# A decoder layer with Strassen products: the up blocks of the feed-forward part taken product by product

## What is computed

```python
h = rmsnorm(x, pre_ffn_g[l])
up = causal_depthwise_conv(h @ w_up[l], conv_w[l], conv_b[l])   # w_up: 2048 x 2*5632, conv of 3 taps
gate, val = jnp.split(up, 2, axis=-1)
y = (jax.nn.gelu(gate, approximate=True) * val) @ w_down[l]     # w_down: 5632 x 2048
x = x + rmsnorm(y, post_ffn_g[l])
```

## Time and profile before

| | |
|---|---|
| median of 3 runs | 2533.48 us |
| profiled execution: its own time | 2530.21 us |
| profiled execution: span, first to last instruction | 2528.3 us |
| mean granted clock of TensorE | 0.999 |
| TensorE matmuls, busy | 15762, 2511.4 us (99%) |
| DVE busy | 2075.4 us (82%), 2517 instructions |
| ACT busy | 1333.5 us (53%), 1690 instructions |
| feed-forward stretch 1321.8 to 2391.8 | PE 1069.38, DVE 971.85, ACT 615.73 of 1070.00 us; DMA share 0.64 |

### The profile page before, as it was taken

How to read it: one execution, slowest core, us unless ns; L and a number is a source line. 1 busy time by engine, 2 the same in 40 slices (tenths; PEclk the granted TensorE clock), 3 DMA queues, 4 the chain that set the end, 5 groups by cost and what they waited for, 6 DMA issues and landing times. The chain is left out here.

```text
span 2528.3 us, 40321 instructions
## 1 busy us (share of the span) xinstructions
PE 2511.4 (99%) x15762; PEld 2271.4 (90%) x15762; DVE 2075.4 (82%) x2517; ACT 1333.5 (53%) x1690; POOL 185.0 (7%) x271
## 2 busy tenths in 40 slices
PE   9999999999999999999999999999999999999998
PEld 8888888888888888888999999999999999999997
DVE  8898888888888545436898989898999989898987
ACT  8554545555555322325555656555555555565544
POOL 0100000000000000000000101100000000001122
PEclk9999999999999999999999999999999999999999
DMA  6434343333344733434234566666666666666888
GB/s 253 151 124 143 124 136 113 109 121 117 103 158 132 291 99 126 157 128 173 75 101 167 167 175 173 177 173 172 176 165 166 167 166 161 166 167 160 257 234 290
DMA packets 106765, 405.42 MB, mean 160 GB/s; under 512 B 12432, under 2 KB 12448, under 8 KB 100960
## 3 DMA queue, kind: packets, MB, share of 16 engines
q1 hardware_dynamic: 72576, 263.76, 31.7%
q0 software_dynamic: 33728, 138.71, 21.4%
q10 hardware_dynamic: 288, 0.52, 0.1%
HBM read 303.33 MB, written 95.42 MB: 158 GB/s over the span
## 5 line engine op out<-in xcount | busy, mean ns | idle before, releaser
L922 PE MATMUL ps<-h_both,w_hl 128*128 128x256 f32 (+1 forms) x1360 | 416.3, 306 | 0.8 <-DVE w_hl L2777 0.8
L923 PE MATMUL ps<-h_both,w_hl 128*128 128x256 f32 (+1 forms) x1360 | 415.4, 305 | 0.0
L924 PE MATMUL ps<-h_both,w_hl 128*128 128x256 f32 (+1 forms) x1360 | 415.4, 305 | 0.0
L1813 ACT ACTIVATE w_hl<-w_raw 128x768 fp32r<-128x768 f32 x168 | 142.3, 847 | 339.6 <-PE ps L924 339.6
L1109 PE MATMUL ps<-rm_both,w_hl 128*128 128x512 f32 x896 | 315.4, 396 | 1.4 <-DVE w_hl L2262 0.8
L922 PEld LDWEIGHTS ps<-h_both,w_hl 128*128 128x128 f32 x1360 | 259.8, 191 | 13.5 <-DVE w_hl L2777 1.2
L924 PEld LDWEIGHTS ps<-h_both,w_hl 128*128 128x128 f32 x1360 | 259.8, 191 | 11.4
L923 PEld LDWEIGHTS ps<-h_both,w_hl 128*128 128x128 f32 x1360 | 259.9, 191 | 10.9
L922 PE MATMUL ps<-w_hl,h_both 128*128 128x512 f32 (+1 forms) x684 | 261.9, 383 | 1.1 <-issue 0.6
L923 PE MATMUL ps<-w_hl,h_both 128*128 128x512 f32 (+1 forms) x684 | 261.2, 382 | 0.0
L924 PE MATMUL ps<-w_hl,h_both 128*128 128x512 f32 (+1 forms) x684 | 261.0, 382 | 0.0
(11 more groups left out here) (387 smaller groups left out, 6462.7 us busy)
## 6 DMA issues: line engine op xcount, KB each, us to landing
w_raw<-in_w SPq DMA_DIRECT2D x487, 512.0 KB, 3.9
y_scratch<-work POOLq DMA_DIRECT2D x78, 512.0 KB, 9.6
y_scratch<-forms_f POOLq DMA_DIRECT2D x29, 512.0 KB, 13.3
y_scratch<-big POOLq DMA_DIRECT2D x27, 512.0 KB, 7.7
gate_scratch<-mixing POOLq DMA_DIRECT2D x8, 1024.0 KB, 6.0
mixing<-in_x POOLq DMA_DIRECT2D x4, 1024.0 KB, 7.0
mixing<-mixing POOLq DMA_DIRECT2D x16, 256.0 KB, 3.7
merged<-gate_scratch POOLq DMA_DIRECT2D x4, 1024.0 KB, 12.6
```

The lines of the kernel that those rows point to most:

```text
L922: pe.matmul(bank, s_hi, m_hi_, start=first, stop=False, skip_group_check=skip)
L923: pe.matmul(bank, s_hi, m_lo_, start=False, stop=False, skip_group_check=skip)
L924: return pe.matmul(bank, s_lo, m_hi_, start=False, stop=last, skip_group_check=skip)
L1813: act.activation(hi[:, 0:RAW_W], w_raw[:, i % RING, HB:], ACT.Copy).then_inc(hi_ready, 1)
```

## The change

The up blocks of subs 1 to 21 take the form of the W blocks, and with it the weight stream of these subs is packed as there (8 chunks of the same size: two of each quarter). A sub has 14 forms f = 0 to 13, in the order P1, Q5, Q6, Q3, Q7, P2, Q4, two of each product (half of the depth each); w_hl holds four forms, each good for 16 matmuls. `t_one` to `t_four` on DVE make the summed forms, of 1024 columns: into down_sum (SBUF) for the first half, and into bank pair 0 of PSUM for the second. ACT's `up_seed` copies x to y, and `up_half_*` copy out the left halves of the banks; DVE adds the right halves in eight steps. Form f + 4 takes the slot of form f.

Down block: the third sum goes to bank pair 0 and waits until ACT has taken product 1 out, not until product 3 is done; raw slots are given back by the right sum (two) and the third sum, not by the lo of k = 4 and 6; bank pairs and slots are renumbered. Plain down blocks use other banks for sub 21.

```diff
+            def up_half_form(s, f):
+                p, a, slot = CHAIN[f // 2], f % 2, slots_of(s)[f % RING]
...
+                pe.wait_ge(*up_lo_made(s, f))
+                if p == P1 and a == 0:
...
+                        pe.wait_ge(*pair_left(s, "x"))
...
+                if p == Q6 and a == 0:
+                    pe.wait_ge(up_seeded, s)
+                if p == Q3 and a == 0:
+                    pe.wait_ge(u_step, 6 * s - 5)
+                if p == Q7 and a == 0:
+                    pe.wait_ge(u_step, 6 * s - 4)
+                if p == Q4 and a == 0:
+                    pe.wait_ge(u_step, 6 * s - 2)
+                for kk in range(4):
...
+                    for m in range(2):
...
+                        pe.matmul(bank.rearrange("p (a s) -> p a s", a=2), w_hl[:, slot, 0, c], operand_both(p, k), ...)
+                        mm = pe.matmul(bank[:, 0:HB], w_hl[:, slot, 1, c], o_h, start=False, stop=k == KH - 1, ...)

 ACT
+            def up_half_q5(s):
+                act.wait_ge(*up_used(s, form_at(Q5, 1)))
+                act.wait_ge(v_tap0, s * 2)
+                act.activation(uc22, sum_halves(chain_banks(s)[2])[0], ACT.Copy).then_inc(up_half, 1)
...
+            def ups(s, tasks):
+                for f in range(2, FORMS):
+                    if f == 5:
+                        up_seed(s)
+                    if f == 7:
+                        up_half_q5(s)
+                    if f == 9:
+                        up_half_x2(s)
+                    up_hi(s, f)
+                    if f in tasks:
+                        tasks[f]()
+            def odd_tasks(g):
+                return {2: lambda: val_linear(g, 0), 5: lambda: gate_linear(g, 0), 9: lambda: gelus(2 * g)}
...
                 leave_product(g, e, 3)
-                sum_form_hi(g, e, 6)
-                quad_hi(c, PER_HALF, c + PER_HALF - 1)
-                quad_sum_hi(n + PER_HALF, PER_HALF)
+                sum_form_hi(s, 6)
+                up_hi(s + 1, 0)
                 leave_product(g, e, 4)
+                up_hi(s + 1, 1)
                 leave_product(g, e, 5)
-                quad_hi(c, PER_HALF + 1, c + PER_HALF)
-                quad_sum_hi(n + PER_HALF + 1, PER_HALF + 1)
                 leave_product(g, e, 6)
                 if e:
                     gate_linear(g, e)
+                    quad_half(g, 0, {2: lambda: val_linear(g - 1, 1), 4: lambda: gelus(2 * g - 1),
+                                     7: lambda: first_forms_hi(g - 1, half_chunk_0(g, 0)),
+                                     11: lambda: second_form_hi(g - 1), 12: lambda: third_forms_hi(g - 1)})

 DVE
+            def third_sum(s):
+                w = s - 2
+                dve.wait_ge(y_left, left_before(w) + 4)
+                dve.wait_ge(sum_ready, sums_before(s) + 2 + 6)
+                TTm(up_t[1], down_sum, down_raw(s, B21), ALU.subtract).then_inc(lo_ready, 1)
...
+            def ups(s, tasks, start=2):
+                for f in range(start, FORMS):
+                    if f == 7:
+                        up_q5(s)
+                    if f == 9:
+                        up_x2(s)
+                    if f == 11:
+                        up_c12_first(s)
+                    if f == 12:
+                        up_c22_first(s)
+                        up_c12(s)
+                        up_c22(s)
+                    up_lo_of(s, f)
+                    if f == 0:
+                        up_t_one(s, 0)
+                    if f == 2:
+                        up_t_one(s, 1)
+                    if f in (3, 4):
+                        up_t_two(s, f - 3)
+                    if f in (6, 7):
+                        up_t_three(s, f - 6)
+                    if f in (10, 11):
+                        up_t_four(s, f - 10)
+                    if f in tasks:
+                        tasks[f]()
+            def odd_tasks(g):
+                return {3: lambda: val_taps(g, 0, (1,)), 4: lambda: val_taps(g, 0, (0,)),
+                        6: lambda: gate_taps(g, 0, (1,)), 8: lambda: gate_taps(g, 0, (0,)),
+                        10: lambda: products(2 * g, 0)}
...
             def quad_half(g, e, tasks):
+                s = 2 * g + e
+                ups(s, tasks)
+                first_sum(s)
+                raw_form_lo(s, 0)
+                up_c11(s)
+                raw_form_lo(s, 1)
+                raw_form_lo(s, 2)
+                up_c21(s)
+                sum_form_lo(s, 3)
+                second_sum(s)
+                right_sum(s)
+                sum_form_lo(s, 4)
+                third_sum(s)
+                sum_form_lo(s, 5)
+                up_lo_of(s + 1, 0)
+                sum_form_lo(s, 6)
+                up_t_one(s + 1, 0)
+                up_lo_of(s + 1, 1)
                 if e:
                     gate_taps(g, e)
```

More of the change, by code:

```diff
@@ L112, in half_chunk_0, with up_base, downs_before, sums_before @@
     return C_LOOP + PER_HALF * half_index(g, e)
-def sums_before(g, e):
-    w = half_index(g, e)
-    return KH + PER_HALF * min(w, QUAD_HALVES) + KH * max(w - QUAD_HALVES, 0)
+def up_base(s):
+    return half_chunk_0(s // 2, s % 2) if s > 1 else C_SUB1
+def downs_before(s):
+    return min(max(s - 2, 0), QUAD_HALVES)
+def sums_before(s):
+    return 2 * (s - 1) + 6 * downs_before(s)
+def sum_his_before(s):
+    return 6 * (s - 1) + 4 * downs_before(s)
+def slots_of(s):
+    v = (0, 1, 2, 3)
+    for n in range(2, s + 1):
+        if n == 2 or n - 3 >= QUAD_HALVES:
+            v = v[2], v[3], v[0], v[1]
+        else:
+            v = v[3], v[2], v[0], v[1]
+    return v
+def down_slots(w):
+    v = slots_of(w + 2)
+    return v[2], v[3], v[0], v[1], v[2], v[0], v[1]
 def splits_before(g):
@@ L1963, in _ @@
                 r_split(2 * (j - RING), 2 * (j - RING) + 2)
-            for i in range(2):
-                quad_hi(C_SUB1, i, C_SUB1 - 2 + 2 * i)
-                quad_sum_hi(i, i)
-                if i == 0:
-                    act.wait_ge(r_lo, 4 * TT)
-                    for t in range(4):
-                        bank = done(A, FFN_USE, t, C_SUB1)
-                        dst = (u_gate, u_val)[t // 2][:, t % 2, :]
-                        act.activation(dst, bank, ACT.Copy).then_inc(plain_left, 1)
@@ L1974, in quads @@
-            def quads(c, n, tasks):
-                for i in range(2, KH):
-                    quad_hi(c, i, c + (i - 1))
-                    quad_sum_hi(n + i, i)
-                    if i in tasks:
-                        tasks[i]()
-            quads(C_SUB1, 0, {2: lambda: gate_linear(0, 0), 3: lambda: val_linear(0, 0), 4: lambda: gelus(0)})
-            quad_hi(C_LOOP, 0, C_LOOP - 1)
-            quad_sum_hi(KH, 0)
-            leave_p1(1)
-            quad_hi(C_LOOP, 1, C_LOOP)
-            quad_sum_hi(KH + 1, 1)
@@ new lines, in _ @@
+            up_hi(1, 1)
+            act.wait_ge(r_lo, 4 * TT)
+            for t in range(4):
+                bank = done(A, FFN_USE, t, C_SUB1)
+                dst = (u_gate, u_val)[t // 2][:, t % 2, :]
+                act.activation(dst, bank, ACT.Copy).then_inc(plain_left, 1)
+            def ups(s, tasks):
[9 more added lines that the diff above has]
+                        tasks[f]()
@@ L2820, in down_raw, with up_raw, up_lo_of @@
-            def down_raw(c, slot):
-                dve.wait_ge(raw_full[slot], (c // RING + KH // RING) * 16 + 16)
+            def up_raw(s, k):
+                c = up_base(s) + k
+                dve.wait_ge(raw_full[c % RING], c // RING * 16 + 16)
+                return w_raw[:, c % RING, :]
+            def up_lo_of(s, f):
+                p, slot = CHAIN[f // 2], slots_of(s)[f % RING]
+                hi, lo = w_hl[:, slot, 0, :].bitcast(F32), w_hl[:, slot, 1, :]
+                dve.wait_ge(*up_hi_made(s, f))
+                if p in RAW_PLACE:
+                    src = w_raw[:, (RAW_PLACE[p] + f % 2) % RING, :]
+                else:
+                    src = w_raw[:, f % 2, :] if p == Q7 else up_t[f % 2]
+                if p in (Q6, Q7):
+                    i = STT(lo, src, -1.0, hi, ALU.mult, ALU.subtract)
+                else:
+                    i = TTm(lo, src, hi, ALU.subtract)
+                i.then_inc(up_lo_made(s, f)[0], 1)
```

640 lines of the change are left out of this document (326 added, 314 removed).

## The result

The changed kernel takes 2640.25 us (median of 4 runs, 2638.63 to 2640.75); the kernel before took 2533.14 on the same chip. The ratio is 1.0419, 95% interval 1.0406 to 1.0432: slower by 4.2%. The forecast of 2596 us had the direction and the main mechanism, waits for queues in the wrong order; 2640 lies 44 us above it and 5 us above its range, because three terms of the sum were off. The profiled execution of the changed kernel has a span of 2638.8 us, that of before 2528.3.

A forecast was written before the change was run, and what follows sets the result against it. TensorE, busy 99% of the span, was taken as the bound. Queue waits less the 1.50 us gain, taken as 3.5 us for 18 halves, added 63 to 2530.2: 2593 us profiled, median about 2596, range 2550 to 2635.

The forecast's parts named there:

- What bounds it, and DVE's fill: Whole kernel: TensorE, busy 99% of the span, bounds it; DVE would have 56.3 us of work in an even half of 57.9.
- The gain on TensorE: Up blocks: 112 pairs at 346.6 ns replace triples at 360 ns, saving 1.50 us a sub, 31 us over 21 subs.
- What the order of the queues makes of it: Feed-forward halves: TensorE waits for DVE's and ACT's queues and hidden transfers, mean loss 4.35 to 6.3 us a half.
- Rival 5: Halves: TensorE's clock falls in the waits, a half loses several us more, total above 2640 us; chance 0.03.
- Subs 1, 20 and 21: Outer subs: a gain of 4.5 us against waits of the same kind, −4 to +9 us, taken as 0.
- The sum: Whole kernel: 18 halves at 3.5 us net loss give +63 us, so 2593 us profiled and a median of about 2596.
- rival 2: Halves: DVE's lead covers even halves, about half the waits stay, 2534 us and up to 2560; chance 0.12.
- Rival 1: Halves: the queues keep TensorE fed and the full 31 us are gained, 2502 us; chance 0.16.
- Rival 4: Up blocks: a pair costs what the triple costs, waits come without the gain, 31 us more, 2627 us; chance 0.04.
- Rival 3: Every half: stores and loads pile up, 2 to 4 us more than taken, 2630 to 2670 us; chance 0.06.

The follow-up runs named there:

- r1: The changed kernel with the same instructions, tiles and banks, but other orders on ACT and DVE from sub 1's end to sub 20: 2545.7 us.
- r2: r1 with the merging of passes undone in the up blocks, three passes of 256 columns: 2560.7 us.
- e2: The changed kernel with accumulating stores writing 8 columns of each product tile instead of 1024, most of the feed-forward sum left out: 2612.7 us.
- r5: A mended version of r1's reordering, with 8 columns of each accumulated product tile stored instead of 1024 (most of the sum left out): 2522.6 us.
- e1: The changed kernel with the first two gate taps of odd halves moved behind up_q5 on DVE: 2632.8 us.
- e4: The changed kernel with the third down sum back in its form's own room, behind the low part of form 5: 2640.5 us.
- e5: The changed kernel with the edits of e1 and e2 together (most of the sum left out): 2605.4 us.
- e6: The changed kernel with the seed and Q5's half eviction with its sum one form earlier, on ACT and DVE: 2633.0 us.
- r8: A third queue order of the changed kernel's instructions, with the narrow pass of each pair first but for each product's first k: 2521.5 us.

## Why the prediction was right, and where it was wrong

**What bounds it, and DVE's fill.** Right: 56.27 us of DVE work in the even half (56.3 forecast), no wait of over 0.15 us before down products (0.2 forecast before the sixth, 0.26 by the starts), the sums in PSUM take 1.23 us (1.218 taken).

**The gain on TensorE, 1.50 us a sub.** Wrong by half, and the first step that failed. It measured 0.75 (r1 and r2), and up blocks without a wait take 39.56 us, not 38.82. The fault is the row chosen for it. In the profile of the changed kernel a W block, whose instructions the change does not touch, goes from here to here:

```profile
723.58 0.40 PE L1191 MATMUL ps<-h_both,w_hl 128*128 128x512 f32 x1
...
763.15 0.40 PE L1191 MATMUL ps<-h_both,w_hl 128*128 128x512 f32 x1
```

39.57 us, where the profile of before had 38.82. A pair has two spacings, 346.6 and 353.3 ns, and I took one block for the price. No second profile was needed to see it. The trace of before has both: of its 203 unbroken stretches of 8 W pairs, 120 go at the faster spacing and 20 at the slower (the rest take 355 ns a pair or more, waits among them). From the first to the second of these rows, where weights and tokens change sides, it makes 61 pairs in 21.56 us, 353.4 ns each; 8 of the 20 have the sides of the up blocks:

```profile
342.13 0.40 PE L1109 MATMUL ps<-w_hl,rm_both 128*128 128x512 f32 x1
...
363.69 0.40 PE L1109 MATMUL ps<-w_hl,rm_both 128*128 128x512 f32 x1
```

Over 18 halves that is up to 13.5 us. Setting the trace above the page was right all the same: the Trainium skill (TensorE: Matmul & The Clock Gate, Back-to-back issue gap) gives a warm matmul by itself 2.5 ns beyond its columns, and says that in a stream with weight loads both operations set the spacing. Here, with a weight load for each matmul, a pair takes 26.6 to 33.3 ns more than the 320 ns of its columns at 2.4 GHz.

**What the order of the queues makes of it.** Right in kind and sum, and in place for the even half. Forecast for the mean half: 4.35 to 6.3 us of waits, 5.0 taken. Measured over the 17 halves, by the starts: 4.6 us in waits of over 0.1 us and 0.7 in smaller delays. In single halves: waits of 0.34, 0.52, 1.33, 0.77, 1.28, 0.24 and 0.96 us before forms 2, 3, 4, 5, 6, 8 and 12 of the even half shown, by the starts on the timeline, 5.4 in all (forecast 5.5 to 6.7, form by form 0.5, 0.7, 1.6, up to 1.2, 1.2, then 1.3 for the rest); 0.71, 2.83 and 1.16 before forms 4, 5 and 6 of the odd one, 4.7 (forecast 3.2 to 5.9). In the odd half the share was wrong: I put 2.7 us before form 6 and 0.4 before form 5. The late load of chunk 5 (8.0 us, within my 7.1 to 8.9) moved the larger wait one form ahead, and up_q5's shrank behind it. Without the transfers, in e2, up_q5's wait is 2.6 us by the starts, where I had laid out 2.7.

**Rival 5, the clock, at a chance of 0.03.** It came true in part, and is the second step that failed: the sum has the clock's cost at nothing. From sub 3 on nine waits, of 2.2 to 3.0 us by the starts, were followed by a slow stretch (0.77 to 0.80 in the one shown) of 1.5 us extra each on average, 13 in all. I had read the clock of the last 28 us and used it for a rival only, not for a term of the sum; the waits that I forecast were of the length at which it shows.

**Subs 1, 20 and 21, −4 to +9, taken as 0.** The third: they cost some 10 us, just past the upper bound, and sub 2, one of the 18 halves, cost 6.9 where 3.5 was taken. Sub 1 has a wait of 2.0 us and sub 2 one of 3.2, each with a slow stretch at it, and in sub 20 the combining sums stand in DVE's queue beside everything else. I had listed them and not laid them out.

**The sum.** A half cost 5.3 us more than before, not 3.5: the gain is 0.75 smaller, the clock costs 0.8 on average, waits and small delays are 0.3 more. For 17 halves that is 31 us, with 3.4 for sub 2 and 10 for subs 1, 20 and 21 makes 44: 2596 + 44 = 2640, as measured. The pairs or the clock alone, put into the upper bound, would have brought the time into the range; the outer subs were in it already. One sum in the chances is off by a hundredth: a third of rival 2's 0.12 is 0.04, not 0.03.

**Rival 1**, the full gain, is out as the kernel stands, and at the spacing that most blocks take even an order without waits does not win 31 us: r5's halves are 0.75 us under before's, 1.1 with the narrow pass first. **Rival 4** was half true. **Rival 3**, transfers pile up in every half, is out: in even halves e2 took away 0.3 us on average, and the median landing of a load over 1400 to 2290 us is 4.3 us as before.

## What to carry to other kernels

When a step is cut into smaller pieces, the queues that feed it are due more often, and an order that was good for the large pieces has to be laid out anew: here the same instructions took 2640 us in one order and 2517 in another. A list of waits tells who was last; moving what it names mostly moves the wait. And a price read from one block should be read in other blocks of the same trace, and in a second profile, before it is multiplied by 21.

## What the runs showed of the hardware that was not expected

*A wait can cost more than itself.* From sub 3's start on, the changed kernel and e1, e2, e4, e5 and e6 have between them some 50 waits of TensorE of 2.1 us or more, by the starts; 32 of them are followed by a granted clock near 0.8 and mostly 1.1 to 1.7 us of extra time (2.9 in three cases), and none of the some 220 between 0.9 and 2.1 us is. That is no threshold: in sub 1, waits of 2.0 us before form 6 were followed by it in the changed kernel, e4 and r1 and not in e2, and in sub 2 one of 3.2 us was not in e2 and e5. Which of the long ones are was not found out: in e2 waits of the same 2.58 us were followed by it in 3 cases of 9.

*A pair of passes has more than one spacing.* From r5, a slow block and then a fast one, and last the narrow pass first, from r8:

```profile
1759.96 0.40 PE L1356 MATMUL ps<-h_both,w_hl 128*128 128x512 f32 x1
1760.20 0.28 PE L1358 MATMUL ps<-h_both,w_hl 128*128 128x256 f32 x1
1760.32 0.40 PE L1356 MATMUL ps<-h_both,w_hl 128*128 128x512 f32 x1
...
2055.60 0.39 PE L1356 MATMUL ps<-b_both,w_hl 128*128 128x512 f32 x1
2055.83 0.28 PE L1358 MATMUL ps<-b_both,w_hl 128*128 128x256 f32 x1
2055.94 0.39 PE L1356 MATMUL ps<-b_both,w_hl 128*128 128x512 f32 x1
```

```profile
1405.52 0.28 PE L1357 MATMUL ps<-h_both,w_hl 128*128 128x256 f32 x1
1405.64 0.40 PE L1358 MATMUL ps<-h_both,w_hl 128*128 128x512 f32 x1
1405.88 0.28 PE L1357 MATMUL ps<-h_both,w_hl 128*128 128x256 f32 x1
```

Where nothing waits, a block stays at one spacing, 39.56 or 38.86 us. Forms behind a wait can go on at the other one (346 ns a pair behind form 8's 0.4 us in sub 6 of r1), or not; and in r5 one block of 17 runs at 38.86 with no wait listed before it. With the narrow pass first all blocks without a wait took 39.2 to 39.3. The 13 ns that I took for "what a matmul costs beyond its columns" are thus no constant. What sets the spacing stays open.
